# Second mixer of a two-block network: GpSimd's share handed to VectorE and ScalarE, jobs made of head pairs, gate columns as outputs

## The reference

```python
def second_block(x, ...):
    for l in range(DEPTH):                              # DEPTH = 2
        h = rms_norm_2(x, norm_mix_pre[l])
        a_q, a_kv, a_gate, d_q, d_kv, b_in, c_in = jnp.split(h @ w_in[l], splits, axis=-1)
        o_cmp, p_cmp = nsa_compressed_attention(qa, k_cmp, v_cmp)
        o_slc = nsa_selected_attention(qa_rot, ...)      # 8 heads of 64, 2 key heads
        o_win = banded_attention(qa_rot, ..., NSA_WINDOW, None)
        ga = jax.nn.sigmoid(a_gate)                      # 24 columns: 3 gates x 8 heads
        o_a = ga[0] * o_cmp + ga[1] * o_slc + ga[2] * o_win
        o_b = conformer_conv(b_in, ...)                  # 31 taps, 512 channels, layer norm
        o_c = pool_mixer(c_in, ...)                      # window means of 2, 4, 8, 16 tokens
        o_d = banded_attention(qd, ..., SWA_WINDOW, swa_sinks[l])   # 8 heads
        up = jnp.einsum("bsnc,ncd->bsnd", stack(o_a, o_b, o_c, o_d), w_branch[l])
        gates = jax.nn.sigmoid(h @ w_gate[l])            # 4 x 1024
        x = x + rms_norm_2(sum_n(gates * up) @ w_o[l], norm_mix_post[l])
        x = x + rms_norm_2(conv_ffn(x), norm_ffn_post[l])
    return x
```

## Time and profile before

| | us |
|---|---|
| median of 3 runs (lowest, highest) | 2386.15 (2383.81, 2387.85) |
| the profiled execution | 2386.95 |
| its span | 2385.1 |
| second mixer, layer 0, by the timeline | about 1185 to 1560 |
| second mixer, layer 1 | about 1790 to 2173 |

### The profile page before, as it was taken

The page is one execution under the profiler, slowest core; times in us unless marked ns, Lnnn a source line. Parts: engine busy times, 40 slices in busy tenths (PEclk is TensorE's granted clock), DMA queues, the critical chain, the costliest instruction groups (busy, mean ns, idle before and its releaser), DMA issues.

```text
span 2385.1 us, 41025 instructions
## 1 busy us (share of the span) xinstructions
PE 2274.3 (95%) x17996; PEld 2178.3 (91%) x18000; DVE 1512.0 (63%) x1755; ACT 1057.7 (44%) x1236; POOL 465.7 (20%) x305
## 2 busy tenths in 40 slices
PE   8999999999999999999999988999999898899998
PEld 7999989999999988999998887889989888788998
DVE  5546656555655755745569895567765988555765
ACT  4434345443544444543432534355552253445553
POOL 2002311000100421100023443200002344320100
PEclk8999999999999999999998999999999899999999
DMA  7555434555555542555543433435544343334652
GB/s 236 181 190 167 155 104 147 195 186 186 176 195 177 176 133 98 174 197 179 184 144 107 142 109 104 143 134 193 185 132 144 106 142 114 107 116 135 202 192 74
DMA packets 285011, 367.25 MB, mean 154 GB/s; under 512 B 9970, under 2 KB 257698, under 8 KB 284578
## 3 DMA queue, kind: packets, MB, share of 16 engines
q1 hardware_dynamic: 281106, 361.01, 45.8%
q10 hardware_dynamic: 3728, 3.62, 0.5%
HBM read 363.56 MB, written 1.05 MB: 153 GB/s over the span
## 4 chain that ended last, share of the span: by engine, by line
PE 80%; DVE 11%; ACT 5%; issue 2%; POOL 1%; DMA 1%; ACTq 0%; POOLq 0%; DVEq 0%
PE ps L576 23%; PE ps L577 22%; PE ps L578 22%; DVE sq L2300 3%; ACT whi L1200 2%; DVE wlo L1730 2%; PE ps L661 1%; PE ps L660 1%; PE ps L659 1%; PE ps L620 1%; PE ps L1026 1%; PE ps L852 1%; PE ps L826 1%; PE ps L1005 0%; DVE sq L2296 0%
## 5 line engine op out<-in xcount | busy, mean ns | idle before, releaser
L576 PE MATMUL ps<-hhi,whi 128*128 128x256 f32 x3792 | 1084.7, 286 | 33.5 <-DVE wlo L1730 6.0
L578 PE MATMUL ps<-hhi,wlo 128*128 128x256 f32 x3792 | 1075.6, 284 | 0.0
L577 PE MATMUL ps<-hlo,whi 128*128 128x256 f32 x3792 | 1069.0, 282 | 0.0
L1730 DVE TENSOR_TENSOR wlo<-raw,whi 128x2048 fp32r<-128x2048 f32 (+1 forms) x311 | 709.1, 2282 | 443.1 <-ACT whi L1200 443.1
L1200 ACT ACTIVATE whi<-raw 128x2048 fp32r<-128x2048 f32 (+1 forms) x347 | 650.5, 1881 | 689.0 <-PE ps L578 590.1
L576 PEld LDWEIGHTS ps<-hhi,whi 128*128 128x128 f32 x3792 | 727.4, 192 | 50.1 <-issue 13.0
L577 PEld LDWEIGHTS ps<-hlo,whi 128*128 128x128 f32 x3792 | 720.0, 190 | 3.6 <-issue 3.3
L578 PEld LDWEIGHTS ps<-hhi,wlo 128*128 128x128 f32 x3792 | 717.1, 189 | 0.0
L576 PE MATMUL ps<-hidhi,whi 128*128 128x256 f32 x1056 | 297.9, 282 | 1.0 <-DVE hidlo L2072 1.0
L577 PE MATMUL ps<-hidlo,whi 128*128 128x256 f32 x1056 | 298.6, 283 | 0.0
L578 PE MATMUL ps<-hidhi,wlo 128*128 128x256 f32 x1056 | 296.5, 281 | 0.0
(11 more groups left out here) (281 smaller groups left out, 2602.6 us busy)
## 6 DMA issues: line engine op xcount, KB each, us to landing
raw<-in_ffn_w_up SPq DMA_DIRECT2D x88, 1024.0 KB, 5.1
raw<-in_w_in SPq DMA_DIRECT2D x68, 1024.0 KB, 5.2
raw<-in_ffn_w_down SPq DMA_DIRECT2D x66, 1024.0 KB, 4.8
raw<-in_ffn_w_gate SPq DMA_DIRECT2D x43, 1024.0 KB, 5.1
raw<-in_w_gate SPq DMA_DIRECT2D x32, 1024.0 KB, 5.4
raw<-in_w_branch SPq DMA_DIRECT2D x16, 1024.0 KB, 4.9
raw<-in_nsa_cmp_w SPq DMA_DIRECT2D x8, 1024.0 KB, 5.4
raw<-in_w_out SPq DMA_DIRECT2D x6, 1024.0 KB, 4.8
```

Source lines behind the costliest of these rows:

```text
L576: pe.matmul(o, w_hi, m_hi, start=start, stop=False, skip_group_check=True)
L577: pe.matmul(o, w_hi, m_lo, start=False, stop=False, skip_group_check=True)
L578: return pe.matmul(o, w_lo, m_hi, start=False, stop=stop, skip_group_check=True)
L1730: dve.tensor_tensor(wlo[:, slot, 0:n], raw[:, slot, 0:n], whi[:, slot, 0:n].bitcast(F32), ALU.subtract) \
```

## The change

It concerns the second mixer alone, in both layers. (1) `by_pool` is gone: DVE does the subtraction for every unit, as first thing of an iteration (in a branch iteration behind the branch). (2) The cosine products and the window sums move from POOL to DVE, the window sums to iteration 12. (3) `normalize` moves from POOL to ACT, where it stands at the head of iteration i for the job scored at i-2, ahead of `turned` and of the hi split. (4) In a branch iteration `denominators` stands before the branch instead of behind it. (5) A job from 4 on is now a pair of heads (one per half of the array) with one of the two kinds of scores, and PE alternates the halves in scores and value products. (6) The 24 gate columns are computed as outputs (24 rows by 256 tokens, 24 products) and turned by two transposes after unit 16; their sigmoid moves from ACT's iteration 15 to 17. POOL keeps three small fills per mixer.

```diff
-        def by_pool(i):
-
-            return i % RING == 0 and RING < i < M2_END and i != M2_GATE - 1 or i % RING == 1 and M2_GATE < i <= LN_AT + 3
+        def job_of(j):
+            return (j, 2) if j < SWA_JOBS else ((j - SWA_JOBS) // 2, (j - SWA_JOBS) % 2)
...
@@ tensor: scores
-                    for i in range(2):
-                        h = 2 * j + i if j < SWA_JOBS else j - SWA_JOBS
-                        lane = slice((h % 2) * DH, (h % 2) * DH + DH)
...
+                    c, kind = job_of(j)
+                    for t, keys in ((1, SEQ), (0, P)):
+                        for i in range(2):
+                            lane = slice(i * DH, i * DH + DH)
+                            q = (dqr if j < SWA_JOBS else qr)[lane, c, t * P:(t + 1) * P]
...
@@ tensor: unit M2_AG
-                            project_tokens(slot, 0, 24, 24, bank(b, 0, TT * 24).rearrange("p (t n) -> p t n", t=TT)) \
-                                .then_inc(used[slot], 1)
+                            for k in range(KC):
+                                w = slice(k * 3 * NSA_H, (k + 1) * 3 * NSA_H)
+                                last = mm3(bank(b, 0, SEQ)[0:3 * NSA_H, :], whi[:, slot, w], wlo[:, slot, w], hhi[:, k, :],
+                                           hlo[:, k, :], k == 0, k == KC - 1)
...
@@ scalar
+                def normalize(j):
+                    act.wait_ge(rec2_done, rec_steps(l, j + 1))
+                    for i in range(2):
+                        for t, part in ((0, slice(0, P)), (1, slice(P, 3 * P))):
+                            x = s2[:, j % 2, i, part]
+                            act.activation(x, x, ACT.Copy, scale=rec2[:, j % 2, t, i:i + 1]).then_inc(p2_normed, 1)
...
                     joint = i in second_of
+                    if i - 2 in job_scored:
+                        normalize(job_scored[i - 2])
...
@@ vector: next_split
-                    if by_pool(i + 2):
-                        return
...
@@ vector: turn
+                        dve.tensor_tensor(dst, src, cos2, ALU.mult).then_inc(cos2_done, 1)
...
@@ vector: main loop
+                    if i == POOL_AT - 1:
+                        window_sums()
...
                     if joint:
+                        if i - 2 in job_scored:
+                            denominators(job_scored[i - 2])
                         branch(second_of[i])
                         next_split(i)
-
-                        if i - 2 in job_scored:
-                            denominators(job_scored[i - 2])
```

More of the change, by code:

```diff
@@ L1013, in times_v @@
                         pe.wait_ge(ptc_taken, l + 1)
-                    for i in range(2):
[L1015 to L1027, removed]
+                    c, kind = job_of(j)
+                    lane = slice(2 * c // GRP * DH, (2 * c // GRP + 1) * DH)
+                    o = [bank(7, (c % 2) * SEQ, SEQ)[i * DH:(i + 1) * DH, :] for i in range(2)]
+                    first, final = j < SWA_JOBS, j < SWA_JOBS or kind == 1
+                    if j >= SWA_JOBS and kind == 0:
+                        for i in range(2):
+                            r = (2 * c + i) % GRP
+                            row = slice(r * KVH * CP, (r + 1) * KVH * CP)
+                            pe.matmul(o[i], vb[row, lane], ptc[row, :], start=True, stop=False)
+                    for i in range(2):
+                        pe.matmul(o[i], vt[:, kind, 0, lane], pt2[:, i, 0:SEQ], start=first, stop=False)
+                    for i in range(2):
+                        last = pe.matmul(o[i][:, P:], vt[:, kind, 1, lane], pt2[:, i, SEQ:], start=False, stop=final)
                     last.then_inc(pv2_done, 1)
@@ L1145, in mixer2 @@
                             turn(n, kind, k)
+                    if i == M2_AG + 2:
+                        pe.wait_ge(taken2, l * FILLS + M2_AG + 1)
+                        for t in range(TT):
+                            last = pe.transpose(bank(7, t * 3 * NSA_H, 3 * NSA_H), ga_rows[0:3 * NSA_H, t * P:(t + 1) * P],
+                                                ident[0:3 * NSA_H, 0:3 * NSA_H])
+                        last.then_inc(ga_raw, 1)
                     if i == POOL_AT:
@@ L1670, in mixer2 @@
                 zero(cpad[:, :, 0:CONV_PAD], pads)
[L1672 to L1686, removed]
@@ L1699, in normalize @@
-                def normalize(j):
-                    pool.wait_ge(rec2_done, rec_steps(l, j + 1))
-                    for i in range(2):
-                        for t, part in ((0, slice(0, P)), (1, slice(P, 3 * P))):
-                            x = s2[:, j % 2, i, part]
-                            rec = rec2[:, j % 2, t, i:i + 1].broadcast_to(x.shape)
-                            pool.tensor_tensor(x, x, rec, ALU.mult).then_inc(p2_normed, 1)
-                for i in range(M2_END - 2):
-                    for n, (unit, kind, k) in enumerate(TURNS):
-                        if kind == "q" and unit == i:
-                            cosines(n, k)
-                    if i == M2_POOL + 2:
-                        window_sums()
-                    if i - 2 in job_scored:
-                        normalize(job_scored[i - 2])
-                    if by_pool(i + 2):
-                        split_lo(i + 2)
@@ L2271, in compressed_norm, with window_sums @@
                                           ALU.mult).then_inc(sc_den, 1)
+                def window_sums():
+                    dve.wait_ge(taken2, l * FILLS + M2_POOL + 2)
+                    dve.wait_ge(pads, (l + 1) * 3)
+                    for n, (dst, src, g, w) in enumerate(((pool_a, pool_u, 0, 1), (pool_b, pool_a, 1, 2), (pool_a, pool_b, 2, 4),
+                                                          (pool_b, pool_a, 3, 8))):
+                        if n:
+                            dve.wait_ge(pool_step, l * 4 + n)
+                        a = 2 * w - 1
+                        dve.tensor_tensor(dst[:, g:, a:], src[:, g:, a:], src[:, g:, a - w:PW - w], ALU.add).then_inc(pool_step, 1)
                 def pool_means():
```

44 lines of the change are left out of this document (18 added, 26 removed).

## The result

The changed kernel takes **2408.62 us** (median of 4 runs, 2405.18 to 2411.0), the kernel before on the same chip 2387.0 (2383.81 to 2389.1): ratio **1.0091**, 95% interval 1.0072 to 1.011. It is 0.9% slower; 2407 was forecast, and the range of 2378 to 2432 holds it. The profiled execution of the changed kernel took 2406.61 us, its span 2404.8.

What follows compares the result with a forecast made beforehand. PE was taken as full except where the DVE, ACT and POOL chain is late; the walk's +10.3 us a layer made +20.6 on 2386.95, 2407.6, and 0.8 less against the median: forecast 2407 us, range 2378 to 2432.

Steps and rivals of the forecast that it cites:

- The branches' chain: At the mixer's three branches, tanh, split, subtraction and exponentials delay the branch operation: +7.1, +7.1 and +2.3 us a layer.
- The idle time in every second unit: DVE waits 3.6 us before a subtraction for ACT's scaling, copy and hi split, eight times a layer: 29 us.
- the walk: Layer 0 followed unit by unit, noting how late each point is against before; it ended at +10.3 us a layer.
- The stretch given back: DVE work no longer lengthened beside POOL: 50 us a layer, of which taps 30 and subtractions 3.
- One subtraction costs 5.2 us: Six DVE taps at 1332.25 took 7.62 us, not 2.4, beside one POOL subtraction, so it costs DVE 5.2.
- Rival (a): Released taps win if last takes before branches come over 7 us earlier: -18 us a layer, 2350 us; chance 0.15.
- the term for the shorter PE: Pairs on alternating array halves save PE 1.5 us a job over eight jobs; 3.3 us taken off after the third branch.
- The full factor of two: If different array tiles work fully in parallel, pairs save some 0.3 us more a job, moving the sum 1 us at most.
- The waits at the layer norm: Before the third branch, jobs 8 and 9's scalings and the layer norm on ACT give 2.7 us back.

Runs made afterwards that it cites:

- e1: The changed kernel with ACT's hi split put ahead of the job's scaling and copy, in units that neither open nor close a branch: 2376.59 us.
- e7: The kernel before with the gate columns computed as outputs and nothing else changed: 2385.63 us, ratio 1.0004.
- e12: The changed kernel with ACT's hi split ahead of scaling and copy, and ahead of the four tanh in units that open a branch: 2362.11 us.
- e567: The kernel before with pairs, gate columns and all subtractions on DVE; scaling, cosines, window sums stay on GpSimd, denominators behind the branch: 2366.29 us.
- e4: The changed kernel with the scaling of the probabilities back on GpSimd: 2379.29 us, ratio 0.9977.
- b1: e567 with ACT's hi split first in every unit and ahead of the four tanh: 2347.42 us, ratio 0.9846.
- e67: The kernel before with pairs of heads on alternating halves and gate columns as outputs, no work moved between GpSimd, ACT and DVE: 2368.9 us.
- b3: e67 with ACT's hi split first, as in b1, GpSimd still making 18 subtractions a layer: 2392.03 us, ratio 1.0035.

## Why the prediction was right, and where it was off

**The branches' chain** was the core of the forecast, and it is what the trace shows: 9.62 and 9.65 us from take to branch (9.6 said), PE waiting 6.52 and 6.55 us (7 said). Against before, layer 0 and layer 1 are late at the end of the first branch by 10.2 and 10.2 us (11.1 said), at the start of the second by 7.3 and 7.3 (9.3), at its end by 13.8 and 14.5 (16.6), at the start of the third by 12.6 and 13.7 (13.3), at its end by 15.0 and 17.7 (17.5), at the end of the layer by 7.4 and 10.2 (10.3).

**The idle time in every second unit**: the size is right (3.4 to 4.1 us, 3.6 said) and so is the place. That a stretch (DVE's operations lengthened beside GpSimd) which is gone nearly pays for it held for the walk, from before to after. As a price of its own it was undersized: I worked e1's expectation with 7 us a layer on the path, and by the ratios it was 14.5.

**The stretch given back**, 50 us a layer: by the means of DVE's groups in layer 0, before and after, it is 54. Taps gave back 29.4 us (78.1 to 48.7) and the subtractions 3, as said. The rest, some 21 us, which I could only bound, lies in a few operations that each started beside a GpSimd one; two groups of the kernel before (1190 to 1560 us) give 9 of it; in the changed kernel the first has a mean of 0.29 us and the second of 0.17:

```profile
L2270 DVE TENSOR_TENSOR arena<-arena,consts 128x128 f32<-128x128 f32 x2 | 5.1, 2606 | 0.0
L2282 DVE TENSOR_TENSOR arena<-gates,consts 128x16 f32<-128x16 f32 x4 | 5.1, 1264 | 0.1
```

DVE's busy time agrees: -54 and +47 make -7 a layer, and both layers show -15. e5, which moves the subtractions alone (+41 us a layer), gained 10 us for both layers, waits included.

**One subtraction costs 5.2 us** was a wrong reading of the earlier trace rows. The first three of those six taps, beside the GpSimd scalings ahead of the subtraction, take 2.13 us in place of 1.3, and the one tap beside the subtraction 4.77 in place of 0.48, so the subtraction costs 4.3 and the scalings the rest:

```profile
1332.25 2.13 DVE L2300 SCALAR_TENSOR_TENSOR sq<-arena,par,sq 128x256 f32<-128x256 f32 x3
```

Since both went away with the change, the walk did not suffer from it.

**Rival (a)** listed waits that do go, with the change alone: in the changed kernel those at 1378.68 and 1542.82 have no successor, 1.39 us are left at the second branch's start and 0.43 at the norm's mean. What fails is its condition, that the last take before a branch comes more than 7 us earlier: it does not, and the new waits eat these gains. Only with ACT's order changed, the scaling back on GpSimd and the denominators behind the branch are the branches' waits gone too, in b2, at 2344 us, where (a) had said 2350. That the numbers lie so close is in part chance: (a) counted gate columns that gave nothing and left out pairs that gave 16 us.

**The step that failed** is the term for the shorter PE, which was too small. I took 1.5 us a job for the pairs and 3.3 a layer on the path. In the rows above, three jobs' value products and one job's scores, with the compressed products, go from 10.0 us to 4.9; the stretch shrinks by 3.7 us (33.57 to 29.87); and the pairs alone are worth 16 us for two layers where I counted 6.6. Per job that is 0.93 for the value products, 1.0 for the scores and some 0.3 for the compressed ones, 2.3 in all. The full factor of two, which I had set beside what the Trainium skill's page TensorEngine Tiling (Array Packing), section Key Properties, says of parallel tiles, gave an estimate of 1.8: nearer, and still short. That the pairs gain 16 us was measured with all else as before; in the changed kernel they were not taken out by themselves. In (a) I also gave the gate columns 5 us a layer; e7 shows 0.

**The waits at the layer norm**: 2.7 us were taken for job scalings and the norm together. The wait for the variance alone is 5.85 us, and 3.2 us in e12, so it too hung on ACT's list.

**Outside the mixers** I had no term. The feed-forward part between them added 4.6 us to the difference of the spans, at the lower clock, and the part ahead of the first took 2.4 off. That the two nearly make up the 3.0 us by which the mixers lost less than forecast is luck; 2408.6 against 2407 looks better than the walk was.

**Open**: the 14 us from e567 to e4 are given to the denominators' place by PE's waits; no run moved it alone in that base. Why e1 gained twice as much in layer 1 as in layer 0 is not shown.

## What to carry to other kernels

Handing an idle engine's work to a busier one can be free in work and still cost through order. Here subtractions on DVE gained 4 to 10 us, and scalings in ACT's in-order list cost 27, about half of it because the split that everything waits for stood behind them. Before moving work, write down each engine's list, ask who waits for whose last item, and put the item that another engine awaits first; then measure the parts of such a change apart, for here a gain of 20 us was hidden under a loss of 41. And an order is only good for one division of the work: the one that gains 17 us with DVE subtracting (e567 to b1) costs 23 with GpSimd subtracting (e67 to b3).

## What the runs showed of the hardware that was not expected

A single DVE tap of 0.48 us, started just behind a GpSimd subtraction, lasts 4.81 us; in the changed kernel, with no GpSimd work beside them, all 240 taps average 0.48. Timeline of DVE in b3, narrowed to that tap:

```profile
1354.83 4.81 DVE L2315 SCALAR_TENSOR_TENSOR sq<-arena,par,sq 128x256 f32<-128x256 f32 x1
```

So it is not a slowdown spread over DVE's work, but one instruction that stands until GpSimd's is through (1354.59 + 4.77 = 1359.36). The Trainium skill's page SBUF — State Buffer, section Who interferes with whom, has the loser blocked for the whole instruction; the trace agrees. Not every DVE operation is caught: in the kernel before, eight that read PSUM and the parameters keep their 0.40 us each while GpSimd subtracts for 4.58 us beside them (DVE, then POOL):

```profile
1210.79 2.99 DVE L2189 TENSOR_TENSOR sq<-ps,par 64x240 f32<-64x240 f32 x8 [1.02 <-PE ps L978]
```

```profile
1211.06 4.58 POOL L1685 TENSOR_TENSOR wlo<-raw,whi 128x2048 fp32r<-128x2048 f32 x1 [7.39 <-ACT whi L1200]
```

The short GpSimd scalings of 0.53 us on average cost next to nothing when they fall into DVE's idle time (e4), and about 0.8 us for three taps when they don't.
